# Branch stage and output stage of a hybrid encoder layer in one block: output weights loaded and split beside the last branch products, two row blocks kept in SBUF

## What is computed

```python
y_attn = windowed_gqa_sink(q, k, v, attn_sink) @ w_branch_attn          # 512 -> 1024
y_ssm = s5_bidirectional(u, ..., w_glu, b_glu) @ w_branch_ssm           # ends with y * sigmoid(y @ w_glu + b_glu), 512 -> 1024
merged = g[:, :, 0] * y_attn + g[:, :, 1] * y_ssm                       # g = sigmoid(gates)
x = x + rmsnorm(merged @ w_out, norm_mix_post)                          # 1024 -> 1024
h2 = rmsnorm(x, norm_ffn_pre)
# then the gated feed-forward with a 3-tap convolution, 1024 -> 2816 -> 1024
```

## Time and profile before

| | us |
|---|---|
| median of three runs | 2807.84 |
| the profiled execution's own time | 2807.01 |
| its span in the trace | 2805.3 |
| TensorE busy in the span | 2663.7 |
| VectorE busy in the span | 1571.6 |

### The profile page before, as it was taken

One profiled execution on the slowest core, in us unless ns is written; L12 is line 12 of the kernel. 1 busy time (PEld: TensorE's weight loads), 2 busy tenths in 40 slices (PEclk: granted clock), 3 DMA queues, 4 the chain that ended last, 5 costly groups with the idle time before them and its releaser, 6 DMA issues.

```text
span 2805.3 us, 34566 instructions
## 1 busy us (share of the span) xinstructions
PE 2663.7 (95%) x12486; PEld 2188.4 (78%) x12486; DVE 1571.6 (56%) x1951; ACT 919.6 (33%) x1554; POOL 857.3 (31%) x1076
## 2 busy tenths in 40 slices
PE   7998999999999799979989999979999999999998
PEld 7886788788887577858868888868888877887886
DVE  5102664678798074444576677787776663224333
ACT  5221655621211160023453333343333342113221
POOL 2173330088784000002234444334334420001111
PEclk9999999999999999989999999999999999999999
DMA  6463325454526653454534222222222245335563
GB/s 217 97 253 77 74 71 157 129 182 138 184 93 202 130 190 128 187 173 148 162 96 150 83 83 90 68 68 91 68 86 88 84 153 149 103 87 174 167 174 109
DMA packets 368240, 362.02 MB, mean 129 GB/s; under 512 B 50529, under 2 KB 307041, under 8 KB 363873
## 3 DMA queue, kind: packets, MB, share of 16 engines
q1 hardware_dynamic: 311136, 262.53, 31.6%
q10 hardware_dynamic: 47104, 49.86, 5.3%
q0 software_dynamic: 9856, 47.72, 5.0%
HBM read 248.38 MB, written 111.67 MB: 128 GB/s over the span
## 4 chain that ended last, share of the span: by engine, by line
PE 41%; DMA 5%; issue 5%; DVE 4%; POOL 1%; ACT 1%; ACTq 0%; POOLq 0%; SPq 0%; DVEq 0%
PE tl_banks L406 9%; PE tl_banks L408 9%; PE tl_banks L407 9%; PE tl_banks L110 4%; PE tl_banks L112 4%; PE tl_banks L111 4%; DMA out<-dn_rows 2%; DMA dn_w_raw<-in_w_ffn_down 1%; DVE gu_b_lo L1244 1%; DMA dn_rows<-x_mid 1%; DVE dn_rows L475 1%; DMA ou_w_raw<-in_w_out 1%; DVE dn_f_lo L1352 1%; PE tl_banks L906 0%; DVE gu_a_lo L1238 0%
## 5 line engine op out<-in xcount | busy, mean ns | idle before, releaser
L406 PE MATMUL tl_banks<-gu_b_hi,gu_a_hi 128*128 128x512 f32 x1232 | 483.6, 393 | 28.6 <-DVE gu_gate L1295 18.5
L407 PE MATMUL tl_banks<-gu_b_hi,gu_a_lo 128*128 128x512 f32 x1232 | 482.3, 391 | 0.0
L408 PE MATMUL tl_banks<-gu_b_lo,gu_a_hi 128*128 128x512 f32 x1232 | 482.0, 391 | 0.0
L406 PEld LDWEIGHTS tl_banks<-gu_b_hi,gu_a_hi 128*128 128x128 f32 x1232 | 233.0, 189 | 80.0 <-issue 22.2
L110 PE MATMUL tl_banks<-dn_w_hi,dn_f_hi 128*128 128x512 f32 x704 | 275.4, 391 | 10.8 <-DVE dn_f_lo L1352 5.1
L111 PE MATMUL tl_banks<-dn_w_hi,dn_f_lo 128*128 128x512 f32 x704 | 274.7, 390 | 0.0
L112 PE MATMUL tl_banks<-dn_w_lo,dn_f_hi 128*128 128x512 f32 x704 | 274.6, 390 | 0.0
L408 PEld LDWEIGHTS tl_banks<-gu_b_lo,gu_a_hi 128*128 128x128 f32 x1232 | 233.1, 189 | 48.8
L407 PEld LDWEIGHTS tl_banks<-gu_b_hi,gu_a_lo 128*128 128x128 f32 x1232 | 233.2, 189 | 48.5
L1238 DVE TENSOR_TENSOR gu_a_lo<-gu_raw,gu_a_hi 128x512 fp32r<-128x512 f32 x220 | 193.9, 882 | 99.6 <-ACT gu_a_hi L1047 99.6
L1047 ACT ACTIVATE gu_a_hi<-gu_raw 128x512 fp32r<-128x512 f32 x220 | 138.4, 630 | 243.6 <-PE tl_banks L408 236.6
(11 more groups left out here) (295 smaller groups left out, 5471.5 us busy)
## 6 DMA issues: line engine op xcount, KB each, us to landing
dn_f_raw<-f SPq DMA_DIRECT2D x64, 704.0 KB, 5.8
gu_raw<-in_w_ffn_gate SPq DMA_DIRECT2D x44, 512.0 KB, 3.8
gu_raw<-in_w_ffn_up SPq DMA_DIRECT2D x44, 512.0 KB, 3.8
gs_w_raw<-in_w_in SPq DMA_DIRECT2D x40, 512.0 KB, 4.3
gates<-gs_gate_out ACTq DMA_DIRECT2D x64, 256.0 KB, 2.8
br_rows<-gates POOLq DMA_DIRECT2D x16, 1024.0 KB, 7.0
f<-gu_conv SPq DMA_DIRECT2D x11, 1025.0 KB, 5.3
f<-gu_conv SPq DMA_DIRECT2D x11, 1023.0 KB, 5.6
```

The source lines that it names most:

```text
L406: pe.matmul(out, w_hi, x_hi, start=first, stop=False, skip_group_check=again)
L407: pe.matmul(out, w_lo, x_hi, start=False, stop=False, skip_group_check=again)
L408: return pe.matmul(out, w_hi, x_lo, start=False, stop=last, skip_group_check=again)
```

## The change

`stage_branches` is gone; its work is the function `branches`, called inside the block of `stage_tail`, so no pool ends and no barrier stands between the branches and the output stage. All branch tiles get fixed places in the same region. What is y (four tiles now, `br_y0` to `br_y3`) becomes the place of the raw output weights once the gated y has been split; the attention tiles become the place of the weights' high and low parts.

- SyncE issues the eight output weight loads one after each of the branch weight loads 9 to 16. The y chunks 1 to 3 come in twelve loads of 256 KB instead of three of 1 MB.
- y chunks and attention chunks are split in four instructions of 128x512 instead of one of 128x2048, on ScalarE and on VectorE.
- The sum of the two branches is made per chunk (four adds of 128x512, into the ssm rows) instead of once per row block (128x2048).
- ScalarE splits the eight weight pieces after the last attention product, behind the store of row block 5. VectorE makes four of the low parts between the chunks of block 18, and two each behind chunks 0 and 1 of block 19; behind chunk 2 it makes the low part of token tile 0.
- Tile 0 and tile 1 take k-steps 0 to 5 from DRAM (`first_raw`, row blocks 0 to 5) and k-steps 6 and 7 from the sums in SBUF. From tile 2 on all eight come from DRAM, as before, in loads that wait for the last store.
- The two gain loads and the residual rows are issued after the last product is done and the last store has landed.

```diff
+class OutWeights:
...
+    def split_hi(self, act, k):
+        act.wait_ge(self.w_in[k], 16)
+        act.activation(self.hi[k][:], self.raw[k][:], ACT.Copy).then_inc(self.hi_ready, 1)
+
+    def split_lo(self, dve, k):
+        dve.wait_ge(self.hi_ready, k + 1)
+        dve.tensor_tensor(self.lo[k][:], self.raw[k][:], self.hi[k][:].bitcast(F32), ALU.subtract)\
+            .then_inc(self.lo_ready, 1)
+
+    def split_first_hi(self, act, merged_ready):
+        act.wait_ge(self.first_in[0], 16)
+
+        act.wait_ge(self.lo_ready, 4)
+        act.activation(self.first_hi[:, 0:KD - 2], self.first_raw[:, 0], ACT.Copy).then_inc(self.first_hi_ready, 1)
+        for n in range(2):
+
+            act.wait_ge(merged_ready, (KD - 2 + n) * CHUNKS + 1)
+            act.activation(self.first_hi[:, KD - 2 + n], self.last[n][:, 0], ACT.Copy).then_inc(self.first_hi_ready, 1)
+
+    def split_first_lo(self, dve):
+        dve.wait_ge(self.first_hi_ready, 1)
+        dve.tensor_tensor(self.first_lo[:, 0:KD - 2], self.first_raw[:, 0], self.first_hi[:, 0:KD - 2].bitcast(F32),
+                          ALU.subtract).then_inc(self.first_lo_ready, 1)
...
+def branches(nc, m, place, block, banks, o_w, attn_scratch, y_scratch, gate_scratch, w_glu, b_glu, w_attn, w_ssm,
+             merged_scratch):
...
+        for c in range(1, CHUNKS):
+            for k in range(K):
+                sync.dma_start(y[k][:, columns(c)], y_rows[:, k, columns(c)]).then_inc(y_in[c - 1], 16)
...
+        for i in range(5, len(blocks)):
+            load_weights(i)
+            if 9 <= i < 9 + KD:
+
+                sync.wait_ge(gated_lo, K)
+                o_w.load(sync, i - 9)
+
+        for s in range(2):
+            sync.wait_ge(stored[s], 3 * 16)
+        sync.wait_ge(o_w.lo_ready, 2)
+        for t in range(2):
+            sync.dma_start(o_w.first_raw[:, t], o_w.first_rows[t]).then_inc(o_w.first_in[t], 16)
...
+        for n in range(n_out):
+            if n == n_out - 2:
+
+                act.wait_ge(product_done, number[LAST - 2, CHUNKS - 1] + 1)
+                for k in range(KD):
+                    o_w.split_hi(act, k)
+            if n == n_out - 1:
+                o_w.split_first_hi(act, merged_ready)
+            act.wait_ge(merged_ready, (n + 1) * CHUNKS)
+            act.dma_start(merged_rows[n], rows[:, 2 * (n % 2) + 1]).then_inc(stored[n % 2], 16)
...
+                if h:
+                    dve.wait_ge(chunk_free, p + 1)
+                    dve.tensor_tensor(rows[:, 2 * s + 1, columns(c)], rows[:, 2 * s, columns(c)],
+                                      rows[:, 2 * s + 1, columns(c)], ALU.add).then_inc(merged_ready, 1)
+                if i == LAST - 1:
+                    o_w.split_lo(dve, c)
+                if i == LAST and c < 2:
+                    o_w.split_lo(dve, CHUNKS + 2 * c)
+                    o_w.split_lo(dve, CHUNKS + 2 * c + 1)
+                if i == LAST and c == 2:
+                    o_w.split_first_lo(dve)
+            split_weights(i + 2)
+    return product_done, chunk_free, stored
...
-            load_merged(0)
-            load_merged(1)
+
+            sync.wait_ge(product_done_b, PRODUCTS)
+            for s in range(2):
+                sync.wait_ge(merged_stored[s], KD // 2 * 16)
             pn.load_gain(sync)
...
                 s = t % 2
-                if t >= 2:
+                if t == 1:
+                    act.wait_ge(product_done_b, PRODUCTS)
+                    act.wait_ge(o_w.first_in[1], 16)
+                    act.activation(g_hi[:, s, 0:KD - 2], o_w.first_raw[:, 1], ACT.Copy)
+                    act.activation(g_hi[:, s, KD - 2], o_w.last[0][:, 1], ACT.Copy)
+                    act.activation(g_hi[:, s, KD - 1], o_w.last[1][:, 1], ACT.Copy).then_inc(g_hi_ready, 1)
+                    return
...
             act.sem_inc(d_y_done, 2)
-            for k in range(KD):
-                act.dma_start(o_w_raw[k][:], o_w_rows[k]).then_inc(o_w_in[k], 16)
-            split_merged_hi(0)
-            for k in range(KD):
-                act.wait_ge(o_w_in[k], 16)
-                act.activation(o_w_hi[k][:], o_w_raw[k][:], ACT.Copy).then_inc(o_w_hi_ready, 1)
             split_merged_hi(1)
```

More of the change, by code:

```diff
@@ L501, in __call__, with __init__, load @@
         return self.nc.alloc_sbuf_tensor_at(name, shape, dt, offset=self.at + first)
-def stage_tail(nc, merged_scratch, w_out, gain, x, x_mid, ffn_gain, feat_late, w_gate, w_up, conv_w, conv_b, f_scratch,
+class OutWeights:
+    def __init__(self, m, place, w_out, merged_scratch):
+        raw = [32768, 36864, 65536, 69632, 90112, 94208, 122880, 126976]
+        hi = [40960 + 4096 * k for k in range(6)] + [73728, 77824]
+        lo = [98304 + 4096 * k for k in range(6)] + [131072, 135168]
+        self.raw = [place(f"ou_w_raw{k}", raw[k], [P, D]) for k in range(KD)]
+        self.hi = [place(f"ou_w_hi{k}", hi[k], [P, D], F32R) for k in range(KD)]
+        self.lo = [place(f"ou_w_lo{k}", lo[k], [P, D], F32R) for k in range(KD)]
+        self.first_raw = place("ou_first_raw", 32768, [P, 2, KD - 2, P])
+        self.first_hi = place("ou_first_hi", 65536, [P, KD, P], F32R)
+        self.first_lo = place("ou_first_lo", 69632, [P, KD, P], F32R)
+        self.last = []
+        self.rows = w_out.rearrange("(k p) n -> k p n", p=P)
+        merged = merged_scratch.rearrange("(k p) (t c) -> t p k c", p=P, c=P)
+        self.first_rows = [merged[t][:, 0:KD - 2] for t in range(2)]
+        self.w_in = [m.sem(f"ou_w_in{k}") for k in range(KD)]
+        self.hi_ready = m.sem("ou_w_hi_ready")
+        self.lo_ready = m.sem("ou_w_lo_ready")
+        self.first_in = [m.sem("ou_first_in0"), m.sem("ou_first_in1")]
+        self.first_hi_ready = m.sem("ou_first_hi_ready")
+        self.first_lo_ready = m.sem("ou_first_lo_ready")
+    def load(self, sync, k):
+        sync.dma_start(self.raw[k][:], self.rows[k]).then_inc(self.w_in[k], 16)
+    def split_hi(self, act, k):
[16 more added lines that the diff above has]
+                          ALU.subtract).then_inc(self.first_lo_ready, 1)
+        for n in range(2):
+            dve.wait_ge(self.first_hi_ready, n + 2)
+            dve.tensor_tensor(self.first_lo[:, KD - 2 + n], self.last[n][:, 0],
+                              self.first_hi[:, KD - 2 + n].bitcast(F32), ALU.subtract).then_inc(self.first_lo_ready, 1)
@@ L511, in stage_tail @@
         feat_raw = place("feat_raw", 0, [P, KD, HALF])
[L514 to L519, removed]
+        o_w = OutWeights(m, place, w_out, merged_scratch)
+        o_w_hi, o_w_lo, o_w_lo_ready = o_w.hi, o_w.lo, o_w.lo_ready
         g_raw = place("ou_g_raw", 149504, [P, 2, KD, P])
@@ L687, in stage_tail @@
         block = ctx.enter_context(nc.Block())
+        product_done_b, chunk_free, merged_stored = branches(
+            nc, m, place, block, banks, o_w, attn_scratch, y_scratch, gate_scratch, w_glu, b_glu, w_attn, w_ssm,
+            merged_scratch)
+        PRODUCTS = 4 * (SSM // P) + 2 * KD * CHUNKS
         @block.sync
```

436 lines of the change are left out of this document (216 added, 220 removed).

## The result

The changed kernel takes 2787.34 us in the median of four runs (2785.81 to 2791.61), the kernel before, run four times in all, 2807.20 us (2802.5 to 2810.18). The ratio is 0.9933, with a 95% interval of 0.9915 to 0.9951: 0.7% faster. The forecast was 2791.6 us with a range of 2785.5 to 2799.

A forecast was written before the change was run, and what follows sets the result against it. TensorE's waits at the seam bound the kernel, measured by when tile 2 starts. Saving 20.1 us, less 4.2 for tile 2's stall and 0.5 for split pieces, gives 15.4 off 2807.0: 2791.6 us, range 2785.5 to 2799.

The forecast's parts named there:

- when tile 2 starts: Seam of branches and output stage: the one measure, 43.9 us from last branch matmul's start to tile 2's start before.
- VectorE's ladder: Blocks 18 and 19: VectorE's multiplies, sums and low parts let tile 0 start at 1212.5, shrinking TensorE's hole 17.2 to 1.8 us.
- The clock: Behind the hole at tile 0: full clock was assumed after 1.8 us idle; a fall would cost 1.5 us.
- Tiles 0 and 1: Output stage: 96 matmuls at 0.227 take 21.8 us, so tile 2 could start at 1234.3, 20.1 us earlier than before.
- Tile 2's own wait: Before tile 2: ScalarE's tap loads cause a stall between 0 and 6.1 us, taken as 4.2 us.
- late bound: Before tile 2: taps end at 1236.7, ScalarE is free at 1233.7, tile 2 starts at 1240.4, a stall of 6.1 us.
- The split pieces: Gated y ahead of block 6: four 128x512 instructions on ScalarE instead of one 128x2048 cost 0.5 us.
- Twelve y loads: y chunks 1 to 3: twelve 256 KB loads instead of three cost 0, since bytes decide and not pieces.
- rival D: Glu part, chunk 3: small y pieces are served one after the other; slower, 2839 us; chance 0.04 with anything like it.
- Rival A: Before tile 2: the taps hold nothing up, tile 2 starts at 1234.3, gain 19.6, time 2787.4 us; chance 0.22.
- Rival B: Seam: late end everywhere, including a gain vector landing about 1237 and tile 2 at 1241; 2795 to 2798 us; chance 0.16.
- Nothing new behind tile 2: After tile 2's start: everything hangs on the same chain as before, shifted; a new hole there would mean wrong.

The follow-up runs named there:

- x1: Changed kernel, but tiles 0 and 1 load all eight k-steps from DRAM after the last store, weights still early; 2800.89 us, ratio to before 0.9983.
- x2: Changed kernel, but output weight loads and splits begin only after the last branch product; 2806.16 us, ratio to before 1.0001.
- e1: Changed kernel, but SyncE issues the four tap loads in the branches instead of ScalarE behind its last store; 2780.93 us in one run.
- b1: Kernel before, with only y chunks 1 to 3 in twelve loads and y and attention splits in four instructions; 2810.05 us in one run.
- e2: Changed kernel, but VectorE makes tile 0's low part one chunk earlier, ahead of weight low parts 6 and 7; 2792.36 us in one run.
- b2_taps: Kernel before, with only the tap loads moved from ScalarE to SyncE, at its fifth tile; 2804.59 us in one run.

## Why the prediction was right, and where it was off

The mechanism held wherever a run tested it, but the time fell into the range's lower part, and not where the forecast had its weight: that was a stall of 2.5 to 6 us before tile 2 and a time of 2789 to 2794, to which it gave a chance of 0.50. Measured are 1.2 us and 2787.34.

- *What bounds the kernel: when tile 2 starts.* Right. The drop in D less 0.2 at block 6 makes 18.6 us; the spans differ by 18.5, and that they come so close is luck (above).
- *VectorE's ladder.* Right: tile 0 was to start 2.0 us after the last branch matmul (1210.5 to 1212.5), it starts 1.96 after it, with an idle of 1.57 released by `ou_first_lo`. The step of 3.6 us a chunk was measured at 3.60.
- *The clock.* Right: 0.47 and then 0.39, granted clock 1.00. What the lower level looks like was seen in x1 and x2 (0.76 us, in x1 then 0.63).
- *Tiles 0 and 1 in 21.8 us.* Right: in e1, where nothing holds tile 2, it starts 21.88 us after tile 0, and D is 20.05 us less than before, where the sum said 20.1.
- *Tile 2's own wait.* This is the step that was mis-sized: 4.2 us forecast, 1.24 measured (by e1's D). Its mechanism was right: the taps hold ScalarE longer than before (14.1 us, not 9.7), and e1 takes the wait away. That the hold grew because other transfers run beside the taps was argued, and no run isolates it. The 4.2 itself came from no row; it was chosen between the bounds of 0 and 6.1. The late bound took two things from rows that don't carry over. It let ScalarE come free 3.0 us before the last taps land; in the changed kernel it came free 6.0 before (issue at 1216.42, 13.9 us to landing, so 1230.3, against 1224.34). And it let them land at 1236.7, which in the positions of after, whose last branch matmul is 4.43 us earlier, is 1232.3; they landed at 1230.3. The two take 5.0 us off the late bound of 6.1, which leaves 1.1. By choosing 4.2 I had taken off 1.9 of them. One reading under it was loose as well: in the earlier trace rows the DMA share is 9, 5, 8 and 7 tenths from 1240 to 1244 while the rate is 4 to 69 GB/s, and not 9 throughout.
- *The split pieces.* +0.5 forecast, 0.2 to 0.3 measured (after, b1): the copy in pieces takes 2.18 us, not the 2.39 of the sigmoids from which I worked it out.
- *Twelve y loads: 0.* Right (b1), and rival D, with the y chunks served one after the other, is out: no wait in chunks 1 to 3.
- *Rival A* (2787.4) has the number of the result, 2787.34, and that is luck: it said that the taps hold nothing up. The true case, 1.24 us, lies between its 0 and the forecast's 4.2, nearer to it. With 1.24 for 4.2 and 0.2 for 0.5 the sum is 18.7 us and 2788.3, against 2788.49 of the profiled execution.
- *Rival B's gain vector* is out: without 4 MB of weights in front, the two gain loads land in 4.9 and 6.4 us, not 15.3.
- *Nothing new behind tile 2.* Right, no wait is new there, but I hadn't allowed for what the table shows: with no edit in it, the stretch behind tile 2 varies by 5 us, which is a quarter of the whole effect.

## What to carry to other kernels

A hole between two stages has several chains in it, and removing one shows the next: x1, with the weights ready, still waits 12.3 us where before waited 17.2, x2, with two k-steps kept on the chip, waits 19.7, and with both edits the wait is 1.57. Take the small waits in the order of the chain: the ladder's order was worth nothing while the taps set the end, and 1.85 us once they were gone. And a position in one trace carries over to the next only from a common event; measured from the last matmul ahead of the seam, an edit worth 1.24 us could be read from one run, while the spans of single runs differ by more than that with no edit at all.

## What the runs showed that I had not expected

- Four loads of 11 KB, gathered element by element, held ScalarE for 14.1 us where they stood behind a 1 MB store and beside other loads. Issued by SyncE in the branches (e1), they held SyncE for 7.1 us (1044.86 to 1051.97), the first three landed in a median of 5.4 us, and nothing waited for them.
- How long TensorE idles doesn't by itself say whether the clock falls. At the seam, a hole of 3.00 us (e2) was followed by matmuls at the lower level, holes of 1.57 and 1.08 (after) and of 1.62 (before) were not. Further on, holes of nearly one length, at the same place in the program, went either way. Of before, at two places of the feed-forward part (tiles `gu_...` and `dn_...`):

```profile
1895.07 0.47 PE L406 MATMUL tl_banks<-gu_b_hi,gu_a_hi 128*128 128x512 f32 x1 [2.48 <-issue]
...
2338.99 0.50 PE L110 MATMUL tl_banks<-dn_w_hi,dn_f_hi 128*128 128x512 f32 x1 [3.73 <-DVE dn_f_lo L1352]
```

And of the changed kernel:

```profile
1870.56 0.47 PE L406 MATMUL tl_banks<-gu_b_hi,gu_a_hi 128*128 128x512 f32 x1 [2.49 <-issue]
...
2316.62 0.80 PE L110 MATMUL tl_banks<-dn_w_hi,dn_f_hi 128*128 128x512 f32 x1 [4.24 <-DVE dn_f_lo L1681]
```

Before ran on at full clock behind both. The changed kernel ran eight matmuls at the lower level from the fourth one on behind its 2.49 us (1871.38 to 1874.74), and twelve behind its 4.24 us (2316.62 to 2321.88, with a granted clock of 0.68 from 2318 to 2324). The longer second hole isn't the reason either: b2_taps has 3.67 us there and falls, e1_taps has 3.62 and doesn't.

These places hold most of what the span behind tile 2 has more. Measured from the start of tile 2, the changed kernel is 1.3 us ahead of before at the first hole, 0.9 behind at the second, 3.3 behind after the twelve matmuls, and 4.7 at the end. The eight matmuls cost 1.5 us (3.36 against 1.82 at full clock) and the twelve 2.4 (5.26 against 2.85 for before's twelve); the last 1.5 us I haven't placed. The same shows in a stretch of 140 us around the second hole, at the same distance from tile 2, with 13 matmuls fewer and a granted clock of 0.96 against 0.99. Of before:

```profile
2260.00:2400.00 140.00, 131.59 (x569) 107.17 (x568) 61.61 (x58) 40.27 (x41) 14.93 (x12) 0.99 0.49 148
```

And of the changed kernel:

```profile
2237.00:2377.00 140.00, 131.12 (x556) 106.51 (x555) 61.10 (x57) 39.68 (x40) 14.93 (x12) 0.96 0.49 149
```

Why the clock falls in one execution and not in the other is open.
